# Attention scores of a decoder layer: both passes of one block of queries in a row, in place of one pass over all blocks and then the other

## The reference, cut to what matters

```
for i in range(seq // Q_BLOCK):                 # Q_BLOCK = 128: four blocks of queries
    end = (i + 1) * Q_BLOCK
    qb, kb = q[:, :, i * Q_BLOCK:end], k[:, :, :end]          # head_dim = 64
    z = einsum('bhqd,bhkd->bhqk', qb, kb) * scale             # both branches
    z = z + c_q[..., :, None] - c_k[..., None, :]             # fx only
    # sb: sigmoid and cumulated log weights for k_pos < q_pos; fx: softmax for k_pos <= q_pos
```

## Time and profile before

| what | value |
|---|---|
| runs | 758.57, 759.11, 759.6 us (median 759.11) |
| the profiled execution | 759.82 us, of which the span of the core's instructions 758.0 us |
| PE busy | 742.5 us, 98% of the span |
| ACT, POOL, DVE busy | 318.5, 337.1, 358.1 us (42, 44, 47%) |
| mean granted TensorE clock | 0.998 of full speed |

### The profile page before, as it was taken

How to read it: one execution, slowest core, us unless ns; L and a number is a source line. 1 busy time by engine, 2 the same in 40 slices (tenths; PEclk the granted TensorE clock), 3 DMA queues, 4 the chain that set the end, 5 groups by cost and what they waited for, 6 DMA issues and landing times.

```text
span 758.0 us, 9588 instructions
## 1 busy us (share of the span) xinstructions
PE 742.5 (98%) x3520; PEld 621.6 (82%) x3520; DVE 358.1 (47%) x504; ACT 318.5 (42%) x430; POOL 337.1 (44%) x245
## 2 busy tenths in 40 slices
PE   7999999999999999999999999999999999999996
PEld 5888788888888888788899888888888888888884
DVE  3328669869868774355562112212221222221567
ACT  5223485674765765662123323332333243423410
POOL 6545154334434432794005444444444443654800
PEclk9999999999999999999999999999999999999999
DMA  8322412313314213762003232323232327332002
GB/s 294 108 88 101 122 56 80 117 56 116 106 56 118 78 57 111 278 225 80 1 1 112 83 111 83 111 83 111 83 111 83 110 83 271 118 103 91 29 29 83
DMA packets 24477, 78.33 MB, mean 103 GB/s; under 512 B 2944, under 2 KB 3328, under 8 KB 24448
## 3 DMA queue, kind: packets, MB, share of 16 engines
q1 hardware_dynamic: 24448, 77.94, 30.1%
HBM read 71.63 MB, written 2.10 MB: 97 GB/s over the span
## 4 chain that ended last, share of the span: by engine, by line
PE 95%; ACT 1%; DMA 1%; issue 1%; DVE 1%; POOL 0%; SPq 0%; DVEq 0%; POOLq 0%; ACTq 0%
PE ps L972 92%; PE ps L1066 2%; DMA sb_k<-qk_lo 1%; PE ps L1145 0%; DMA w_raw<-w_stream_in 0%; POOL w_lo L413 0%; ACT w_hi L473 0%; ACT fx_p L554 0%; DVE fx_nmax L786 0%; ACT L460 0%; ACT g_all L603 0%; SPq L340 0%; ACT wout_hi L606 0%; DVE x L907 0%; DVE bn_parts L879 0%
## 5 line engine op out<-in xcount | busy, mean ns | idle before, releaser
L413 POOL TENSOR_TENSOR w_lo<-w_raw,w_hi 128x512 fp32r<-128x512 f32 x220 | 294.4, 1361 | 370.7 <-ACT w_hi L473 365.0
L473 ACT ACTIVATE w_hi<-w_raw 128x1024 fp32r<-128x1024 f32 x109 | 115.5, 1060 | 225.8 <-DMA w_raw<-w_stream_in 225.8
L972 PE MATMUL ps<-x1T_hi,w_hi 128*128 128x512 f32 (+1 forms) x376 | 141.3, 376 | 0.0
L972 PE MATMUL ps<-x1T_lo,w_hi 128*128 128x512 f32 (+1 forms) x376 | 141.2, 375 | 0.0
L972 PE MATMUL ps<-x1T_hi,w_lo 128*128 128x512 f32 (+1 forms) x376 | 141.2, 375 | 0.0
L935 DVE SCALAR_TENSOR_TENSOR conv<-ps,col,conv 128x511 f32<-128x511 f32 (+1 forms) x44 | 33.0, 749 | 165.3 <-ACT conv L653 162.3
L972 PE MATMUL ps<-xT_hi,w_hi 128*128 128x512 f32 x264 | 105.9, 401 | 1.4 <-issue 1.0
L972 PE MATMUL ps<-xT_hi,w_lo 128*128 128x512 f32 x264 | 103.2, 391 | 0.0
L972 PE MATMUL ps<-xT_lo,w_hi 128*128 128x512 f32 x264 | 102.9, 390 | 0.0
L972 PEld LDWEIGHTS ps<-x1T_hi,w_hi 128*128 128x128 f32 x376 | 70.8, 188 | 12.9
L972 PEld LDWEIGHTS ps<-x1T_lo,w_hi 128*128 128x128 f32 x376 | 70.8, 188 | 12.7
(11 more groups left out here) (139 smaller groups left out, 1126.3 us busy)
## 6 DMA issues: line engine op xcount, KB each, us to landing
w_raw<-w_stream_in SPq DMA_DIRECT2D x109, 512.0 KB, 3.2
wout_raw<-w_out_in SPq DMA_DIRECT2D x8, 512.0 KB, 4.7
r_raw<-w_stream_in SPq DMA_DIRECT2D x5, 512.0 KB, 9.9
xT_raw<-xT_in SPq DMA_DIRECT2D x8, 256.0 KB, 6.5
x<-x_tok_in SPq DMA_DIRECT2D x4, 512.0 KB, 4.3
ln_rows<-rows_in SPq DMA_DIRECT2D x4, 512.0 KB, 5.5
out_dram<-x SPq DMA_DIRECT2D x8, 256.0 KB, 2.0
sb_q<-sb_q SPq DMA_DIRECT2D x8, 128.0 KB, 2.4
```

The lines of the kernel that those rows point to most:

```text
L413: lo = nc.gpsimd.tensor_tensor(w_lo[:, slot, cs], w_raw[:, slot, cs], plain(w_hi[:, slot, cs]), ALU.subtract)
L473: nc.scalar.activation(w_hi[:, slot, :], w_raw[:, slot, :], ACT.Copy).then_inc(hi_ready, 1)
L972: return nc.tensor.matmul(out_, lhs, rhs, start=start, stop=stop, skip_group_check=True)
```

## The change

In both branches the loop over the blocks of queries becomes the outer one and the loop over the two passes the inner one. The same eight matmuls per branch are issued, with the same operands, the same places in PSUM and the same `start` flags; the waits ahead of them and the mask matmuls behind them stay where they are.

```diff
-                for q, k, first in ((sb_q[e][:], sb_k[e][:], True), (qk_lo[hd, 0, :], sb_k[e][hd, :], False)):
-                    for r in (3, 2, 1, 0):
+                for r in (3, 2, 1, 0):
+                    for q, k, first in ((sb_q[e][:], sb_k[e][:], True), (qk_lo[hd, 0, :], sb_k[e][hd, :], False)):
                         o, width = SB_PS + QUERY_OFF[r], P * (r + 1)
                         product(ps[:, o:o + width], q[:, P * r:P * (r + 1)], k[:, 0:width], start=first and r > 0)
                 masked(SB_PS, MASKED, 0).then_inc(sb_scored, 1)
...
-                for q, k, first in ((q_bias_rows[:, e, :], k_bias_rows[:, e, :], True), (fx_q[e][:], fx_k[e][:], False)):
-                    for r in (3, 2, 1, 0):
+                for r in (3, 2, 1, 0):
+                    for q, k, first in ((q_bias_rows[:, e, :], k_bias_rows[:, e, :], True),
+                                        (fx_q[e][:], fx_k[e][:], False)):
                         o, width = FX_PS + QUERY_OFF[r], P * (r + 1)
                         product(ps[:, o:o + width], q[:, P * r:P * (r + 1)], k[:, 0:width], start=first and r > 0)
                 masked(FX_PS, MASKED, 1).then_inc(fx_scored, 1)
```

## The result

| | before | after |
|---|---|---|
| first comparison, median (range, runs) | 758.75 us (758.28 to 759.6, 6) | 770.58 us (769.26 to 771.9, 6) |
| ratio, 95% interval | | 1.0154 (1.0141 to 1.0166) |
| profiled execution (span) | 759.82 us (758.0) | 769.63 us (767.8) |
| mean granted TensorE clock of the profiled execution | 0.998 | 0.996 |

The change costs 11.8 us. The direction and the mechanism were forecast, the size was not: 770.58 lies 2.6 us above the forecast of 768.0 and 0.6 us above the end of the range. As a difference the miss is 2.9 us: the forecast stood 8.9 us above its base of 759.11, and the six runs of the kernel before have a median of 758.75. A second comparison (the experiment `e9_after_again`) gave 770.32 against 760.17 us, ratio 1.0141 (1.0117 to 1.0164).

What follows compares the result with a forecast made beforehand. PE was taken as the bound. The profiled 759.82 us plus 9.3 us for new row-count changes in sb, less 1.0 us hidden in a wait, gave 768.1; the forecast was 768.0 us, range 762.0 to 770.0.

Steps and rivals of the forecast that it cites:

- What bounds the kernel: Whole kernel: PE, busy 98% of the span, is the bound; its busy time outside the sb scores should not move.
- The fx branch: fx scores, all with 128 partitions: pairs keep 1.22 us per half, taken as 0 change, at most 0.08 us either way.
- The price of a change of the row count: sb scores: six new 128/64-row changes per half at 0.194 us (0.09 drain, 0.104 uncovered load), 9.3 us over eight halves.
- the bounds: Cost of each new sb row-count change: from below 0.03 to 0.13 us by width, from above 0.26; 0.194 taken.
- rival two: sb row-count changes: 0.15 us delay counts from the previous matmul's start, so wide matmuls hide most; 762.6 us, chance 0.07.
- rival three: sb changes from 64 back to 128 rows cost only 0.09 to 0.10 us; about 765.1 us, chance 0.08.
- rival four: sb changes behind wide matmuls: load waits for the previous matmul's shown end, 0.26 us each; 770.8 us, chance 0.05.
- rival five: sb's middle step: 0.14 us comes from returning to block r = 3, gone in pairs; 758.0 us, chance 0.04.
- rival six: sb scores: instruction order doesn't matter, the engine pays once per branch; 759.1 us, chance 0.06.
- The sign: PE timeline, sb scores: loads about 0.32 us after a 512-wide matmul, 0.26 after 384, 0.21 after 256.
- The hidden 1.0 us: PE's wait at fill(0) in h = 2: longer sb scores fill it, hiding 1.0 of that half's 1.16 us.
- The step that failed: The sum: sb drains counted as 9.3 us of PE time, less 1.0 hidden, with no term for the granted clock.

Runs made afterwards that it cites:

- e9_after_again: The changed kernel run once more without alteration, beside the kernel before: 770.32 against 760.17 us.
- e4_passes_128: Kernel before with sb's second pass repeating the 128-row operands of the first (lo by hi left out), so no 64-row matmul: 758.38 us, ratio 0.9992.
- e2_sb_only: Changed kernel's paired order in the sb branch only, fx as in the kernel before: 770.21 us, ratio 1.0144.
- e7_work_in_wait: Changed kernel plus four unused 512-wide matmuls in PE's wait ahead of the first sb scores: 769.56 us, ratio 1.013 to the kernel before.
- e1: Paired order in the fx branch only, sb as in the kernel before: 759.72 against 759.71 us, ratio 0.9999.
- e6: sb in pairs in halves 1 to 7, half 0 and fx as in the kernel before: 767.36 us, ratio 1.0107.
- e3: Changed kernel with sb's second pass repeating the 128-row operands of the first, so no 64-row matmul: 758.0 us, ratio 0.9977 to the kernel before.
- e10: Kernel before with sb in pairs in halves 1 to 7 and four unused matmuls in PE's wait of half 0: 767.92 us, ratio 1.0102.

## Why the prediction was right or wrong

- **What bounds the kernel: right.** PE's own list got longer, and the time with it. PE's busy time outside the sb scores was to stay; of its 11.2 us more, 9.7 are in the scores and 1.4 behind those of half 0, at half clock.
- **The fx branch at nothing: right.** 1.22 us before and after, and 0.9999 for fx alone.
- **The price of a change of the row count: right.** Forecast 0.194 us for each of six new changes, 1.16 us per half, 2.67 us for the scores. Measured 2.69 us, 1.18 more than before, so 0.197 per change and 9.4 us for eight halves against 9.3. The choice between the bounds was right too: the delay counts from the last column (rival two would have 0.15 us behind every width), it is the same on the way back to 128 rows (against rival three), and it doesn't grow with the width (against rival four). `e4_passes_128` took rival five away, `e2_sb_only` rival six. Rival four's 770.8 us is the number nearest to the measured one, and that is luck: it wants 0.26 us per change. The sign as the prediction worded it, a load 0.32 us after the matmul before, isn't what the timeline has: behind a change a matmul is shown from the start of its own load, so the distance reads 0.43 us, 0.104 more, and likewise 0.37 for 0.26 and 0.31 or 0.32 for 0.21.
- **The hidden 1.0 us: right in the profile, not settled for the timed runs.** The wait ahead of `fill(0)` in h = 2 is gone in the trace after; from mask to fill it gave back 1.2 us. But it was read from one execution. In the eight profiles of kernels with sb as passes, or with 128 rows, PE's waits within h = 2 come to between 0 and 1.3 us, and the one ahead of `fill(0)` is in the kernel before alone; in the six with pairs in halves 1 to 7 there is none. So a typical run had less than 1.0 us to give back, and how much isn't measured.
- **The step that failed: the drains were priced as time alone, and the granted clock was not in the sum, a term put at nothing without a reason.** Half 0 has a wait of PE ahead of its sb scores, 0.9 us in the kernel before; the prediction counted only the waits behind the first scores. With 1.2 us more of drains right behind it, the mean clock was low in 18 of 19 runs, and without them in about a quarter. Half 0 alone costs 4.1 us, of which 1.2 are drains; the rest, 2.9 us, goes with the clock, whose 6.8 us at half speed in the profiled execution lose 3.4. In the changed kernel the profiled execution lost about 1.6 us that way: of its 9.8 us over before, the sb scores take 9.7 (8 x 1.18 and 0.2 of the fall), the mask and the fill behind the scores of half 0 another 1.4, and the wait of h = 2 gives 1.2 back. (Half 0 began 0.75 us earlier there, and the rest of the span took that back.) The run of `e9_after_again` that kept its clock took 767.7 us, 0.3 below the forecast of 768.0. What makes the clock fall is not shown, only what makes it more frequent.
- **The remainder.** The drains of 9.4 us less a share of 1.0 us for the wait, and 1.9 to 2.9 us for the clock, give 10.3 to 12.3 us, an estimate; measured were 11.8 and 10.2, one within it and one just below. Some runs of the kernel before have the fall too, which lowers the difference. The difference between these two, on two sets of runs, stays open; the kernel before had more low clocks in the second (nine of 23).

## What to carry to other kernels

Count the changes of a matmul's partition count in a stream, not the matmuls: each costs a drain and an uncovered weight load, here 0.197 us behind a matmul of 256 columns or more, where behind a 128-wide one the kernel before pays 0.14. Group the matmuls of one row count, put the change behind the narrowest, or pad the contraction with zero rows, which here kept the stream distances and gained 0.25%. Where short pauses are added next to a wait that is already there, ask for the granted clock too, and read it from several runs, since one profile of the kernel before did not show what 18 of 63 of its runs had.

## What the runs showed of the hardware that was not expected

- The granted clock falls to 1.2 GHz without any long idle time. In `e7_work_in_wait` PE's only wait there was 0.16 us, and two of the four runs have a low mean clock. It also fell in the old order of the scores, behind waits of 1.2 and 1.7 us (e1, e6), and did not behind 0.9 to 1.3 us (before, e3, e4, e10). In halves 1 to 7 the same scores never had a stretch at half clock, in six profiles. Why half 0 alone is prone to it is open.
- A fall lasted 3.4 us in the changed kernel and twice that with pairs in half 0 alone, where PE had waited 1.5 us ahead of the scores. A mean clock of 0.992, as in that kernel, stands also in one run of the changed kernel and one of `e2_sb_only`.
- A change between 128 and 64 partitions costs the same in either direction, and the same behind 512, 384 and 256 columns (0.197 us within 0.01).
